# Sums of squares and a factor spread, from plain fp32 products to split operands

## The reference

```
def _rmsnorm(x, g):
    xf = x.astype(jnp.float32)
    y = xf * lax.rsqrt(jnp.mean(xf * xf, axis=-1, keepdims=True) + EPS) * g.astype(jnp.float32)
...
q = _rmsnorm(q.reshape(B, S, ATTN_HEADS, HEAD_DIM), q_gain[l])
k = _rmsnorm(k.reshape(B, S, ATTN_HEADS, HEAD_DIM), k_gain[l])
```

## Time and profile before

| | us |
|---|---|
| median of 3 runs | 2680.35 |
| lowest and highest | 2678.11, 2682.05 |
| the profiled execution | 2681.13 |
| its span in the trace | 2679.3 |

### The profile page before, as it was taken

One profiled execution on the slowest core, in us unless ns is written; L12 is line 12 of the kernel. 1 busy time (PEld: TensorE's weight loads), 2 busy tenths in 40 slices (PEclk: granted clock), 3 DMA queues, 4 the chain that ended last, 5 costly groups with the idle time before them and its releaser, 6 DMA issues. The chain is left out here.

```text
span 2679.3 us, 37078 instructions
## 1 busy us (share of the span) xinstructions
PE 2643.3 (99%) x14606; PEld 2290.1 (85%) x14606; DVE 1996.0 (74%) x2349; ACT 1235.8 (46%) x1609; POOL 65.3 (2%) x108
## 2 busy tenths in 40 slices
PE   8999999999999999999998999999999999999998
PEld 6688997777888888888888999999998888888787
DVE  4577645557777776566679888888887988888786
ACT  6322333335544444234556656656655433333332
POOL 0000000000000000000000000000001000000100
PEclk9999999999999999999999999999999999999999
DMA  7478765427555556656763565565568776685843
GB/s 239 140 270 283 256 226 194 137 84 262 189 173 173 173 172 236 197 167 212 258 197 117 191 220 188 183 220 184 186 221 320 255 270 246 217 322 190 300 142 110
DMA packets 319992, 557.18 MB, mean 208 GB/s; under 512 B 19600, under 2 KB 134928, under 8 KB 319312
## 3 DMA queue, kind: packets, MB, share of 16 engines
q1 hardware_dynamic: 289984, 456.19, 51.6%
q0 software_dynamic: 22144, 83.89, 8.5%
q10 hardware_dynamic: 7696, 14.81, 1.5%
HBM read 437.25 MB, written 117.44 MB: 207 GB/s over the span
## 5 line engine op out<-in xcount | busy, mean ns | idle before, releaser
L1270 PE MATMUL main<-sf,f_wh 128*128 128x256 f32 x1728 | 490.1, 284 | 6.4 <-DVE cf_low L2558 3.6
L1271 PE MATMUL main<-sf,f_wh 128*128 128x256 f32 x1728 | 489.7, 283 | 0.0
L1272 PE MATMUL main<-sf,f_wl 128*128 128x256 f32 x1728 | 489.7, 283 | 0.0
L1270 PEld LDWEIGHTS main<-sf,f_wh 128*128 128x128 f32 x1728 | 332.4, 192 | 7.1 <-DVE cf_low L2558 3.8
L1271 PEld LDWEIGHTS main<-sf,f_wh 128*128 128x128 f32 x1728 | 332.5, 192 | 0.0
L1272 PEld LDWEIGHTS main<-sf,f_wl 128*128 128x128 f32 x1728 | 332.5, 192 | 0.0
L463 ACT ACTIVATE w_hi<-w_raw 128x512 fp32r<-128x512 f32 (+1 forms) x184 | 113.4, 617 | 291.4 <-PE main L495 216.4
L470 DVE TENSOR_TENSOR w_lo<-w_raw,w_hi 128x512 fp32r<-128x512 f32 (+1 forms) x184 | 123.4, 673 | 162.8 <-ACT w_hi L463 161.0
L493 PE MATMUL main<-act_hi,w_hi 128*128 128x512 f32 x576 | 232.4, 403 | 9.4 <-DVE w_lo L470 9.3
L1431 ACT ACTIVATE f_wh<-group 128x1024 fp32r<-128x1024 f32 x128 | 135.5, 1061 | 206.5 <-PE aux L1170 91.5
L495 PE MATMUL main<-act_hi,w_lo 128*128 128x512 f32 x576 | 225.3, 391 | 0.0
(11 more groups left out here) (286 smaller groups left out, 6055.5 us busy)
## 6 DMA issues: line engine op xcount, KB each, us to landing
group<-w_ff SPq DMA_DIRECT2D x160, 512.0 KB, 5.1
f1raw<-w_ff SPq DMA_DIRECT2D x128, 512.0 KB, 5.9
sf<-f_dram POOLq DMA_DIRECT2D x56, 1024.0 KB, 9.8
group_g<-w_in SPq DMA_DIRECT2D x100, 512.0 KB, 4.6
w_raw<-w_in SPq DMA_DIRECT2D x88, 512.0 KB, 4.7
f_dram<-piece_hi SPq DMA_DIRECT2D x112, 256.0 KB, 4.1
f_dram<-piece_lo SPq DMA_DIRECT2D x112, 256.0 KB, 5.3
t_dram<-stage POOLq DMA_DIRECT2D x48, 512.0 KB, 4.6
```

Of the source, the lines that this page charges most:

```text
L1270: pe.matmul(part, hi_at(8, k)[:, cols], sh, start=first, stop=False, skip_group_check=True)
L1271: pe.matmul(part, hi_at(8, k)[:, cols], sl, start=False, stop=False, skip_group_check=True)
L1272: mm = pe.matmul(part, lo_at(8, k)[:, cols], sh, start=False, stop=last, skip_group_check=True)
```

## The change

Three things are done differently, and the steps between them are moved:

- Each square is split like the other operands: ScalarE squares, waits for that, and copies into sq_hi; VectorE subtracts to get sq_lo (in place of the square). TensorE sums the two parts in two float32r products of 512 columns. The stationary operand `head` is a window of 16 columns with one column of ones, so head n lands in row n-1 of one bank that all 16 heads accumulate into. In VectorE's program the subtraction stands behind the mask of the same iteration.
- The 16 x 512 sums are copied out by ScalarE at n = 21 and turned by four transposes at n = 22. The later steps move: the mean from 17 to 24, the root from 18 to 24, the factors from 22 to 27, the first diagonals from 24 to 29.
- The k factors are split too, with two diagonals for each tile, and the spread is two float32r products.
- The four semaphores of the natural-order tiles become one, and each of the four squares waits for all four transfers. Four small VectorE instructions ahead of the q projection set up `pick` and `ones_r`.

```
+                        pe.wait_ge(sq_low, n)
+                        head = pick[:, 16 - n:32 - n]
+                        pe.matmul(aux[0:16, 3, :], head, sq_hi[:, (n - 1) % 2], start=(n == 1), stop=False)
+                        pe.matmul(aux[0:16, 3, :], head, sq_lo[:, (n - 1) % 2], start=False,
+                                  stop=(n == 16)).then_inc(sums_done, 1)
-                        token_sums(pe, sq[:, (n - 1) % 2], 4 * (n - 1), 3).then_inc(sums_done, 1)
...
+                    if n == 22:
+                        pe.wait_ge(rows_copied, 1)
+                        for t in range(TT):
+                            mm = pe.transpose(aux[:, 2, 16 * t:16 * t + 16], sum_rows[0:16, t * P:(t + 1) * P],
+                                              cst[0:16, C_ID:C_ID + 16])
+                        mm.then_inc(sums_done, 1)
...
-                pe.matmul(aux[:, 0, :], ones, dk[:, :], start=True, stop=True).then_inc(bcast_done, 1)
+                pe.matmul(aux[:, 0, :], ones_r[:], dk_hi[:], start=True, stop=False)
+                pe.matmul(aux[:, 0, :], ones_r[:], dk_lo[:], start=False, stop=True).then_inc(bcast_done, 1)
...
-                act.wait_ge(nat_landed[t], 16)
+                act.wait_ge(nat_landed, 64)
...
-                    act.activation(sq[:, n % 2], src[:, n % 8, :], ACT.Square).then_inc(qk_squared, 1)
+                    act.activation(sq[:, n % 2], src[:, n % 8, :], ACT.Square).then_inc(sq_full, 1)
+                    act.wait_ge(sq_full, n + 1)
+                    act.activation(sq_hi[:, n % 2], sq[:, n % 2], ACT.Copy).then_inc(qk_squared, 1)
...
+                if n == 21:
+                    act.wait_ge(sums_done, 16)
+                    act.wait_ge(pool_mm, NW)
+                    act.activation(sum_rows[0:16, :], aux[0:16, 3, :], ACT.Copy).then_inc(rows_copied, 1)
...
+            chain.step(dve.memset(pick_raw[:, :], 0.0))
+            chain.wait()
+            chain.step(dve.memset(pick_raw[:, 15:16], 1.0))
+            chain.wait()
+            chain.step(dve.tensor_copy(ones_r[:], ones))
+            chain.step(dve.tensor_copy(pick[:], pick_raw[:]))
+            chain.wait()
...
+            def diagonals_k(h):
+                for t in range(TT):
+                    c = 4 * h + t
+                    dve.tensor_scalar(dk_hi[:, t * P:(t + 1) * P], ident, rk_hi[:, c:c + 1].bitcast(F32), None, ALU.mult)
+                    ins = dve.tensor_scalar(dk_lo[:, t * P:(t + 1) * P], ident, rk_lo[:, c:c + 1], None, ALU.mult)
+                ins.then_inc(diag_ready, 1)
...
+                if n < 16:
+                    dve.wait_ge(qk_squared, n + 1)
+                    dve.tensor_tensor(sq_lo[:, n % 2], sq[:, n % 2], sq_hi[:, n % 2].bitcast(F32),
+                                      ALU.subtract).then_inc(sq_low, 1)
```

More of the change, by code:

```diff
@@ L187, in build @@
         sq = at("sq", [P, 2, S], F32, T)
+        sq_hi = at("sq_hi", [P, 2, S], F32R, T + 4096)
+        sq_lo = at("sq_lo", [P, 2, S], F32R, T)
+        V = T + 14368
+        pick_raw = at("pick_raw", [P, 32], F32, V)
+        pick = at("pick", [P, 32], F32R, V + 128)
+        ones_r = at("ones_r", [P, P], F32R, V + 256)
+        rk_hi = at("rk_hi", [P, 32], F32R, V + 768)
+        rk_lo = at("rk_lo", [P, 32], F32, V + 896)
+        sum_rows = at("sum_rows", [P, S], F32, 192 * KB + 1504)
+        dk_lo = at("dk_lo", [P, S], F32R, T + 8224)
         rB = at("rB", [P, S], F32, T + 10272)
@@ L198, in build @@
         dg = at("dg", [P, S], F32, T + 8224)
-        dk = at("dk", [P, S], F32, 192 * KB + 1504)
+        dk_hi = at("dk_hi", [P, S], F32R, 192 * KB + 1504)
         ident = cst[:, C_ID:C_ID + P]
@@ L226, in build @@
         cst_landed, poolw_landed, ki_doubled = sem("cst_landed"), sem("poolw_landed"), sem("ki_doubled")
-        nat_landed, x_squared = [sem(f"nat_landed{t}") for t in range(TT)], sem("x_squared")
+        nat_landed, x_squared = sem("nat_landed"), sem("x_squared")
+        sq_full, sq_low, rows_copied = sem("sq_full"), sem("sq_low"), sem("rows_copied")
         sums_done, root_done = sem("sums_done"), sem("root_done")
@@ L503, in wait_set @@
                 pe.wait_ge(set_free[parity], n)
[L505 to L510, removed]
         def newton(dve, chain, r, ms, tmp, out):
@@ L550, in load_nat @@
             def load_nat(t):
-                sp.dma_start(x_nat[t][:], x[t * P:(t + 1) * P, :]).then_inc(nat_landed[t], 16)
+                sp.dma_start(x_nat[t][:], x[t * P:(t + 1) * P, :]).then_inc(nat_landed, 16)
             def load_qi(L):
@@ L1398, in _ @@
                         act.wait_ge(sums_done, n - 1)
-                    act.activation(sq[:, n % 2], src[:, n % 8, :], ACT.Square).then_inc(qk_squared, 1)
-                if n == 18:
+                    act.activation(sq[:, n % 2], src[:, n % 8, :], ACT.Square).then_inc(sq_full, 1)
[5 more added lines that the diff above has]
+                    act.activation(sum_rows[0:16, :], aux[0:16, 3, :], ACT.Copy).then_inc(rows_copied, 1)
+                if n == 24:
                     act.wait_ge(ms_ready, 2)
@@ L2025, in _ @@
                                              br_hi[:, gr, :].bitcast(F32), ALU.mult, ALU.subtract).then_inc(a_lo, 1)
-                if n == 17:
-                    dve.wait_ge(sums_done, 16)
+                if n < 16:
+                    dve.wait_ge(qk_squared, n + 1)
+                    dve.tensor_tensor(sq_lo[:, n % 2], sq[:, n % 2], sq_hi[:, n % 2].bitcast(F32),
+                                      ALU.subtract).then_inc(sq_low, 1)
+                if n == 24:
+                    dve.wait_ge(sums_done, 17)
                     by_tile = r4sq.rearrange("p (o t) -> p o t", o=1).broadcast_to((P, 16, TT))
                     chain.step(dve.scalar_tensor_tensor(
-                        ms64.rearrange("p (h t) -> p h t", t=TT), aux[:, 3, 0:64].rearrange("p (h t) -> p h t", t=TT),
+                        ms64.rearrange("p (h t) -> p h t", t=TT), aux[:, 2, 0:64].rearrange("p (t h) -> p h t", t=TT),
                         1.0 / HD, by_tile, ALU.mult, ALU.mult))
@@ L2033, in _ @@
                     dve.tensor_scalar(ms64, ms64, EPS, None, ALU.add).then_inc(ms_ready, 1)
-                if n == 22:
+                if n == 27:
                     dve.wait_ge(root_done, 2)
@@ L2047, in _ @@
                     chain.wait()
-                if n == 24:
-                    diagonals(dve, rqk, 32, dk)
+                if n == 29:
+                    chain.step(dve.tensor_copy(rk_hi[:], rqk[:, 32:64]))
+                    chain.wait()
+                    chain.step(dve.tensor_tensor(rk_lo[:], rqk[:, 32:64], rk_hi[:].bitcast(F32), ALU.subtract))
+                    chain.wait()
+                    diagonals_k(0)
                 if 9 <= n < 13:
@@ L2186, in _ @@
                         dve.wait_ge(bcast_done, 2 + h)
-                        diagonals(dve, rqk, 32 + 4 * (h + 1), dk)
+                        diagonals_k(h + 1)
                 if s == 4:
```

## The result

The kernel grew slower by 0.4%: median 2690.3 us (2687.42 to 2696.04, 6 runs) against 2680.51 (2678.11 to 2682.05, 6 runs), ratio 1.004, 95% interval 1.003 to 1.0049. That is +9.8 us, where +6.8 was forecast. The profiled execution took 2692.82, with a span of 2690.8 against 2679.3.

What follows compares the result with a forecast made beforehand. TensorE, busy 99% of the span, was taken to bound the kernel. Its terms, -6.7 - 3.2 + 0.3 + 13.4 + 3.0 = +6.8 us, put the 2680.35 median at 2687.1, range 2681.7 to 2691.5.

Steps and rivals of the forecast that it cites:

- Sums, -6.7: TensorE, v projection: two split products take 0.45 instead of 0.87 for each of sixteen sums, -6.7 us.
- Stalls, +13.4: TensorE waits for late sq_lo: 6.4, 2.5 and 3.3 us behind masks, 1.2 ahead of unit 9; +13.4 us.
- Clock, +3.0: TensorE at half clock after the long stall and one of the two shorter ones, 1.5 us each, +3.0.
- Spread, -3.2: TensorE, spread of the k factors: 0.45 instead of 0.85 us for each of eight heads, -3.2.
- Transposes, +0.3: TensorE: four small fp32 transposes added once, +0.3 us, bounds 0.1 to 0.87.
- Diagonals: zero: VectorE, after the probabilities: four more diagonals per head, +0.9 us there, half a head early; zero cost, bound +2.
- Setup, 0: VectorE ahead of the q projection: four small instructions, about 0.6 us, swallowed by unit 0's stall; zero, bound +1.
- Landing, 0: ScalarE: squares wait for the last x_nat landing, at most 1.2 us late, covered by splits three units ahead; zero.
- The faster one: VectorE's subtractions in time in all units, only the savings remain: -9.6 us, 2670.7; chance 0.05.
- The not-slower one: Last q/k stage blocks land earlier, shrinking the first stall by up to 3.9 us; at most 2681.7; chance 0.15.
- Rival 1's three drops: TensorE's clock falls after all three stalls in the v projection: +8.3 us, 2688.6; chance 0.13.

Runs made afterwards that it cites:

- e8_changed_again: The changed kernel, unaltered, timed once more beside the kernel with its three waits filled: 2690.6 us, ratio 1.0038 to the kernel before.
- e7_all: As e2_late_both, with VectorE's four setup instructions also moved to unit 10 of the indexer: 2674.4 us, ratio 0.9979 to the kernel before.
- e2_late_both: Changed kernel with TensorE's sums one unit later, subtraction ahead of the mask, first subtraction ahead of the last q/k stage mix: 2674.3 us, ratio 0.9977 to before.
- the filled one: Changed kernel with 24, 10 and 13 extra products put ahead of the sq_lo waits at units 1, 3 and 5: 2687.2 us, again 2688.5.
- e5_sums_only: Changed kernel with the spread put back to plain fp32, one diagonal a tile and one product: 2696.3 us, ratio 1.0059 to the kernel before.
- e1_sub_first: Changed kernel with VectorE's subtraction moved ahead of the mask in the same iteration: 2679.9 us, ratio 0.9997 to the kernel before.
- e6_late_only: Changed kernel with each sum one unit later on TensorE, subtraction still behind the mask: 2678.1 us, ratio 0.9998 to the kernel before.

## Why the prediction was right, and where its sizes were off

The direction, the range (2681.7 to 2691.5) and the mechanism held. By steps:

- **Sums, -6.7.** Held: a unit with its sum takes 3.34, forecast 3.33.
- **Stalls, +13.4.** Held: 5.82, 2.43, 3.23 and, at unit 9, 1.1, in all 12.6, or about 13.2 by starts. The first is shorter than 6.4. From the landing of the stage blocks to the first sum it took 10.1 in both traces (300.03 to 310.10, and 298.03 to 308.10 in e8_changed_again), forecast 9.9; but TensorE was ready for the sum about 4.1 and 4.3 after that landing, and not 3.6 as in the kernel before.
- **Clock, +3.0.** Mis-sized; it measured 5.2 in the profiled execution and 3.1 in the second trace. Two things failed. I counted one of the two shorter waits; the first trace has a drop after both, the second after one. And I took 1.5 for each from a drop that came after the wait had ended. After a wait of 5.8 the clock had already fallen, and products were slow for 3.9 (second trace) to 5.6 from the moment TensorE resumed: 1.7 to 2.5. In the first trace, 2.2 of the missing 3.0 are this term. The rule of the Trainium skill, page "TensorE: Matmul & The Clock Gate", section "Why this matters for your kernels", asks for no long idle gaps between bursts; the long wait agrees with it in both traces. It is no help with the shorter ones: the clock fell after 2.4 us in both, and after 3.2 us in one execution and not in the other.
- **Spread, -3.2.** 2.6 alone. The products themselves save what was forecast: the two take 0.46 (420.19 to 420.65), before 0.85. The step that failed is "Diagonals: zero": it looked only at who asks for the diagonals, and not at the copy queued behind them on VectorE. It cost 0.78, within the bound of 2 that I gave it.
- **Transposes, +0.3.** Held: four starts from 393.82 to 394.0, about 0.3 with the step in and out.
- **Setup, 0.** Held as far as can be told. In the first trace TensorE waits 0.5 and 0.3 for w_lo ahead of unit 0, where the kernel before doesn't, and the first square is 0.9 later. But traces of kernels with the same instructions up to there have the first square anywhere from 301.7 to 303.6 (before 302.6; e8_changed_again, the same kernel, 301.7), so the 0.9 can't be put down to the setup (of the two waits the 0.5 recurs in that second trace); and e7_all, which has the setup elsewhere, was no faster than e2_late_both.
- **Landing, 0.** Held; the first square was 1.4 late and not at most 1.2, and the first spread of the token factors came no later.
- **Rivals.** The faster one (the savings alone, 2670.7) is what e2_late_both approached, with the order changed by hand. The not-slower one, an earlier landing of the last stage blocks, didn't come: VectorE waited 3.93 for them, before 3.91. (In the second trace they landed at 298.03, 1.7 earlier than before, but TensorE was earlier too, and the stall was 5.6.) Rival 1's three drops came true in the profiled execution, and two in the other.

What stays open: the stretch of the sums less the spread comes to +9.8 in the first trace (11.7 less 1.9) and +7.6 in the second (9.4 less 1.8), against 9.8 in the medians. From the last logits to the end, traces of equal code differ by more than what is missing (2104.0 and 2105.8 for the changed kernel, 2104.1 and 2109.4 for the filled one; 2103.2 before), partly by where the clock drops, and I can't say which part of that is the change's.

## What to carry to other kernels

A cheaper form of an operation can need one more partner. Before it goes in, read that partner's order for what is queued ahead, and not its busy share: VectorE at 74% had room, and still cost 11.5 us of waits in three places, each behind a mask, the first behind late stage blocks too. The consumer one step later and the short producer ahead of the long one turned the same change from 0.4% slower to 0.2% faster. When TensorE gets a new wait of a few microseconds, add the slow products after it: 0 to 2.5 us for each in these traces.

## What the runs showed of the hardware

After a wait of 5.8 TensorE's clock was already at half when it resumed, and a unit of 24 products and its sum took 1.7 or 2.5 longer; after one of 6.4 (e5_sums_only) 1.5 longer. So a longer wait didn't cost more: what counted was how much of the drop is left when TensorE resumes. 47 useless products in the three waits took that loss away entirely in the stretch, in both traces. Waits of 2.4 were followed by a drop in all three traces that have them (the two of the changed kernel and e5_sums_only). The wait of 3.2 at unit 5 was followed by one in one of those three, so the same wait can cost 0 or 1.2; the 3.2 of e1_sub_first and the 3.7 of e6_late_only, at their first sum, cost 1.5.
